# Relu tiles of their own for each score of the attention index, moved conv gates, and 68 instead of 60 early expert blocks

## The reference

```python
def conformer_conv(val, glu, conv_w, conv_vec):
    u = val * jax.nn.sigmoid(glu)
    ...
    return jax.nn.silu(layer_norm(y + conv_vec[0], conv_vec[1], conv_vec[2], LN_EPS))
    # its result is multiplied by silu of a third projection, the conv gate

def block(args):                       # dsa_attention, 128 queries
    idx_logits = jnp.einsum('bqhd,bsd->bqhs', qib, kf) * (IDX_HEAD_DIM ** -0.5)
    score = jnp.einsum('bqh,bqhs->bqs', wib * (IDX_HEADS ** -0.5), jax.nn.relu(idx_logits))
    adm = chunk_id[:, None, :] <= cqb[:, :, None]
    score = jnp.where(adm, score, -jnp.inf)
    top_val, top_idx = lax.top_k(score, k_sel)          # k_sel = 128
    ...                                # softmax attention of 16 heads over the chosen keys
```

## Time and profile before

| what | value |
|---|---|
| runs | 3465.48 us median of 3 (3461.9 to 3470.55) |
| profiled execution | 3471.03 us, its span 3468.7 us |
| busy share | PE 91%, DVE 64%, ACT 36%, POOL 25% |
| mean granted PE clock | 0.951 of full speed |

### The profile page before, as it was taken

The page is one execution under the profiler, slowest core; times in us unless marked ns, Lnnn a source line. Parts: engine busy times, 40 slices in busy tenths (PEclk is TensorE's granted clock), DMA queues, the critical chain, the costliest instruction groups (busy, mean ns, idle before and its releaser), DMA issues.

```text
span 3468.7 us, 39991 instructions
## 1 busy us (share of the span) xinstructions
PE 3142.5 (91%) x16218; PEld 2454.1 (71%) x16218; DVE 2206.1 (64%) x3495; ACT 1233.6 (36%) x1788; POOL 864.0 (25%) x540
## 2 busy tenths in 40 slices
PE   6799899997797799979899989979999999999996
PEld 4467677675585466757677778858888888888874
DVE  4689989753759766473679799746664444444445
ACT  3234344333322355323333356522222222222223
POOL 2344433320322211024335522222221111111100
PEclk9889999998898899989999999989999999999998
DMA  5211111325211111222223456665553333333330
GB/s 194 85 65 52 50 50 46 104 92 179 70 67 55 49 37 37 71 75 92 73 91 128 137 168 220 206 206 190 192 182 121 122 120 117 121 122 121 122 103 30
DMA packets 164950, 378.30 MB, mean 109 GB/s; under 512 B 10656, under 2 KB 77216, under 8 KB 164640
## 3 DMA queue, kind: packets, MB, share of 16 engines
q1 hardware_dynamic: 164768, 375.76, 32.2%
HBM read 318.04 MB, written 57.67 MB: 108 GB/s over the span
## 4 chain that ended last, share of the span: by engine, by line
PE 70%; DVE 22%; ACT 3%; DMA 2%; POOL 2%; issue 1%; SPq 0%; DVEq 0%; POOLq 0%; ACTq 0%
PE ps L651 20%; PE ps L653 19%; PE ps L652 19%; DVE rw L1648 5%; DVE oh L2197 2%; PE ps L1050 2%; PE ps L975 2%; PE ps L955 1%; DVE at L1936 1%; DVE ai L1934 1%; POOL wsp L2270 1%; PE ps L965 1%; POOL pk L2368 1%; PE ps L824 1%; DVE oh L2192 1%
## 5 line engine op out<-in xcount | busy, mean ns | idle before, releaser
L651 PE MATMUL ps<-hT,wsp 128*128 128x512 f32 x2120 | 878.5, 414 | 114.9 <-POOL wsp L2270 65.9
L653 PE MATMUL ps<-hT,wsp 128*128 128x512 f32 x2120 | 843.0, 398 | 0.0
L652 PE MATMUL ps<-hT,wsp 128*128 128x512 f32 x2120 | 842.6, 397 | 0.0
L2270 POOL TENSOR_TENSOR wsp<-ring,wsp 128x1024 fp32r<-128x1024 f32 x197 | 487.0, 2474 | 1142.9 <-ACT wsp L1109 1142.8
L651 PEld LDWEIGHTS ps<-hT,wsp 128*128 128x128 f32 x2120 | 408.9, 193 | 235.7 <-issue 79.8
L653 PEld LDWEIGHTS ps<-hT,wsp 128*128 128x128 f32 x2120 | 407.7, 192 | 90.2
L652 PEld LDWEIGHTS ps<-hT,wsp 128*128 128x128 f32 x2120 | 410.2, 193 | 80.4 <-issue 4.1
L2375 POOL TENSOR_TENSOR ex<-ex 128x512 fp32r<-128x512 f32 x128 | 175.4, 1385 | 894.5 <-ACT ex L1465 894.5
L2219 DVE TENSOR_TENSOR xT<-ps,xT 128x512 f32<-128x512 f32 x256 | 175.2, 688 | 285.2 <-PE ps L653 285.1
L1109 ACT ACTIVATE wsp<-ring 128x1024 fp32r<-128x1024 f32 x307 | 317.3, 1050 | 92.8 <-PE ps L653 68.3
L652 PE MATMUL ps<-ex 128*128 128x512 f32 x832 | 324.6, 390 | 0.0
(11 more groups left out here) (371 smaller groups left out, 4643.3 us busy)
## 6 DMA issues: line engine op xcount, KB each, us to landing
ring<-in_eu SPq DMA_DIRECT2D x128, 512.0 KB, 3.2
ring<-in_ev SPq DMA_DIRECT2D x128, 512.0 KB, 3.6
gd<-oh SPq DMA_DIRECT2D x8, 4096.0 KB, 14.4
ex<-gd SPq DMA_DIRECT2D x32, 1024.0 KB, 6.6
ring<-in_ein SPq DMA_DIRECT2D x57, 512.0 KB, 3.2
ring<-in_oin SPq DMA_DIRECT2D x40, 512.0 KB, 3.2
ring<-in_ada SPq DMA_DIRECT2D x37, 512.0 KB, 3.3
ex<-zd SPq DMA_DIRECT2D x15, 1024.0 KB, 9.0
```

The lines of the kernel that those rows point to most:

```text
L651: pe.matmul(out, W[0], R[0], start=first, stop=False)
L652: pe.matmul(out, W[0], R[1], start=False, stop=False)
L653: return pe.matmul(out, W[1], R[0], start=False, stop=last)
L2270: pool.tensor_tensor(s[:, 1, :], raw_of(i), s[:, 0, :].bitcast(F32), ALU.subtract).then_inc(pool_done, G.step("lo", i))
```

## The change

Seven edits. (1) The gates of conv planes 6 and 7 become pieces `late` behind the even output's fence, kept in `ag` and not sent through `yd`; `bgate` 7 is first in step 9. (2) `ybs` writes to tile `ya`, `yas` to tile `hT`, and `yas` k stands between the `lna` pieces; the tables' load is now `tab_in`. (3) Each of the 8 relu results of the index has its own tile; `selb` holds the mask (0 or a large negative number) from the `qi` pieces on and is the first summand, so `pick` has no mask operations. (4) `index` and `pick` of block 0 stand before `value`, those of block b + 1 before the next gate units; q runs one head further ahead. (5) 68 early blocks: three before `hot` 0 instead of one, 27 between `hot` 0 and `hot` 31 instead of 23, six instead of four from the stage's begin on. (6) `z` of units 0 to 3 stands before the last two of them, and each also splits and loads a unit of V. (7) The numbers of `PLACES` are others. The attention's output, the gate's transfers and all else stay.

```diff
--- before.py
+++ after.py
...
-NPRE = 15
+NPRE = 17
+LATE = 6
...
-    "first": (204, 310, 310, 310, 310, 311, 311, 311, 338, 338, 646, 683, 696, 704, 868, 868, 954),
...
+    "first": (135, 392, 392, 450, 593, 593, 679, 699, 699, 699, 879, 879, 927, 965, 976, 976, 976),
...
-        lane = [*(rkv(i) if i <= 7 else gates(range(3)) if i == 8 else gates(range(3, 8))),
+        lane = [*(rkv(i) if i <= 7 else gates(range(3)) if i == 8 else gates(range(3, LATE))),
                 *(x for g in mods.get(i, ()) for x in ada(1, g)),
-                *(dense("bgate", i - 2, 47 + i) if i >= 2 else []), *(conv_in(i + 1) if i <= 6 else [])]
+                *(dense("bgate", i - 2, 47 + i) if 2 <= i < 9 else []), *(conv_in(i + 1) if i <= 6 else [])]
+        if i == 9:
+            lane = [*dense("bgate", 7, 56), *lane]
...
+    order += [("late", m, unit("ein", 16 + m)) for m in range(LATE, 8)]
     order.append(("ybs",))
     order.append(("eb", 0, unit("eout", 1)))
     order.append(("lnm",))
@@ -242,7 +245,9 @@
         if m < 5:
             order.append(("eb", 3 + m, unit("eout", 2 * m + 7)))
         order.append(("lna", m))
-    order.append(("yas",))
+        if m >= 2:
+            order.append(("yas", m - 2))
+    order += [("yas", 6), ("yas", 7), ("tab_in",)]
...
     order.append(("ki", unit("oin", 22)))
+    order += [("qi", m, unit("oin", 18 + m)) for m in range(4)]
     order.append(("wi", unit("oin", 23)))
-    order += [("qi", m, unit("oin", 18 + m)) for m in range(4)]
     order.append(("key", unit("oin", 16)))
+    order.append(("index", 0))
+    order.append(("pick", 0))
     order.append(("value", unit("oin", 17)))
+    g = [0, 3, 7, 11, 16]
     for blk in range(4):
-        order.append(("index", blk))
-        if blk == 3:
-            order.append(("q", 0, unit("oin", 0)))
-        order.append(("pick", blk))
-        order += [("gate", m, unit("oin", 24 + m)) for m in range(4 * blk, 4 * blk + 4)]
+        order += [("gate", m, unit("oin", 24 + m)) for m in range(g[blk], g[blk + 1])]
+        if blk < 3:
+            order.append(("index", blk + 1))
+            if blk == 2:
+                order.append(("q", 0, unit("oin", 0)))
+            order.append(("pick", blk + 1))
+    order.append(("q", 1, unit("oin", 1)))
     for h in range(17):
         if h < 16:
             order.append(("logits", h))
         if h:
             order.append(("pt", h - 1))
-        if h < 15:
-            order.append(("q", h + 1, unit("oin", h + 1)))
+        if h < 14:
+            order.append(("q", h + 2, unit("oin", h + 2)))
...
+    for _ in range(3):
+        pre()
     for tb in range(S // TB):
-        if tb % 4 < 3:
+        if tb % 6 or tb == 30:
             pre()
         order.append(("hot", tb))
+
+    def zs(c):
+        return [("z", c, j, unit("eu", c * JC + j) if c >= NPRE else None) for j in range(JC)]
+
     order.append(("ex_begin",))
-    for _ in range(3):
-        pre()
+    pre()
+    pre()
     order.append(("gload", 0))
     pre()
     order.append(("gload", 1))
+    pre()
+    order.extend(zs(0))
+    pre()
+    pre()
     assert z[0] == NPRE * JC
     first = len(units)
-
-    def zs(c):
-        return [("z", c, j, unit("eu", c * JC + j) if c >= NPRE else None) for j in range(JC)]
-
-    order.extend(zs(0))
     for c in range(NC):
         if c + 1 < NC:
             order.extend(zs(c + 1))
...
+        relu = [*att[4:7], *att[10:14], small[:, :, :].rearrange("p a n -> p (a n)")]
...
+            def late(m, n):
+                w.wait_ge(tensor_done, T("use", n))
+                act.activation(ag[:, m, :], all_b.at[n], ACT.Silu).then_inc(scalar_done, A.step("ag", m))
...
-                    act.activation(hT[:, 0, k, :], yb[:, k, :], ACT.Copy).then_inc(scalar_done, A.step("yb", k))
+                    act.activation(ya[:, 0, k, :], yb[:, k, :], ACT.Copy).then_inc(scalar_done, A.step("yb", k))
...
-            def yas():
-                for k in range(8):
-                    w.wait_ge(pool_done, G("ya", k))
-                    act.activation(ya[:, 0, k, :], yc[:, k, :], ACT.Copy).then_inc(scalar_done, A.step("ya", k))
+            def yas(k):
+                w.wait_ge(tensor_done, T("free", "late"))
+                w.wait_ge(pool_done, G("ya", k))
+                act.activation(hT[:, 0, k, :], yc[:, k, :], ACT.Copy).then_inc(scalar_done, A.step("ya", k))
...
-                    w.wait_ge(vector_done, V.was("acc", (i - 3) // 8, (i - 3) % 8))
-                    act.activation(att[4 + i % 3], all_b.at["ix", blk, h], ACT.Relu, scale=0.125).then_inc(
+                    w.wait_ge(vector_done, V.was("acc", blk - 1, h))
+                    act.activation(relu[h], all_b.at["ix", blk, h], ACT.Relu, scale=0.125).then_inc(
...
+                if c == 0:
+                    hi_to(FIRST + j)
...
+                dve.tensor_scalar(selb[:, m, :], cidr, pcol[:, m:m + 1], NEG, ALU.is_gt, ALU.mult).then_inc(
+                    vector_done, V.step("late", m))
...
                 acc = att[7]
                 for h in range(8):
-                    x, wc = att[4 + (8 * blk + h) % 3], wi[:, blk * 8 + h:blk * 8 + h + 1]
                     w.wait_ge(scalar_done, A("relu", blk, h))
                     own()
-                    if h == 0:
-                        dve.tensor_scalar(acc, x, wc, None, ALU.mult).then_inc(vector_done, V.step("acc", blk, h))
-                    else:
-                        dve.scalar_tensor_tensor(out=acc, in0=x, scalar=wc, in1=acc, op0=ALU.mult,
-                                                 op1=ALU.add).then_inc(vector_done, V.step("acc", blk, h))
+                    dve.scalar_tensor_tensor(out=acc, in0=relu[h], scalar=wi[:, blk * 8 + h:blk * 8 + h + 1],
+                                             in1=acc if h else selb[:, blk, :], op0=ALU.mult, op1=ALU.add).then_inc(
+                        vector_done, V.step("acc", blk, h))
 
             def pick(blk):
-                acc, val, x = att[7], att[8], att[9]
-                dve.tensor_scalar(val, cidr, pcol[:, blk:blk + 1], None, ALU.is_le).then_inc(vector_done, V.step())
-                own()
-                dve.tensor_tensor(acc, acc, val, ALU.mult).then_inc(vector_done, V.step())
-                dve.tensor_scalar(x, val, -1.0, -NEG, ALU.add, ALU.mult).then_inc(vector_done, V.step())
-                own()
-                dve.tensor_tensor(acc, acc, x, ALU.add).then_inc(vector_done, V.step())
+
+                acc, x = att[7], att[9]
                 cur = acc
                 for _ in range(16):
                     own()
@@ -1936,12 +1954,10 @@
                     dve.match_replace(x, m8, cur, -3e38).then_inc(vector_done, V.step())
                     cur = x
                 own()
-                dve.tensor_tensor(x, x, acc, ALU.not_equal).then_inc(vector_done, V.step())
-                own()
-                dve.tensor_tensor(x, x, val, ALU.mult).then_inc(vector_done, V.step())
-                own()
-                dve.tensor_scalar(selb[:, blk, :], x, -1.0, -NEG, ALU.add, ALU.mult).then_inc(
-                    vector_done, V.step("sel", blk))
+                dve.tensor_tensor(x, x, acc, ALU.is_equal).then_inc(vector_done, V.step())
+                own()
+                dve.scalar_tensor_tensor(out=selb[:, blk, :], in0=x, scalar=NEG, in1=selb[:, blk, :], op0=ALU.mult,
+                                         op1=ALU.add).then_inc(vector_done, V.step("sel", blk))
...
+                if m < LATE:
+                    w.wait_ge(ag_in, 16)
+                else:
+                    w.wait_ge(scalar_done, A("ag", m))
...
-                for s in yt_out + ga_out:
+                for s in yt_out:
                     w.wait_ge(s, 64)
-                w.wait_ge(gs_out, 128)
+                for s in ga_out:
+                    w.wait_ge(s, 16 * LATE // 2)
                 for i in range(4):
+                    w.wait_ge(gs_out, 32 * (i + 1))
...
-                sp.dma_start(ag, t["yd"][16:24].rearrange("k p s -> p k s")).then_inc(ag_in, 16)
-
-            def yas():
+                sp.dma_start(ag[:, 0:LATE, :], t["yd"][16:16 + LATE].rearrange("k p s -> p k s")).then_inc(ag_in, 16)
...
+                elif c == 0:
+                    load_to(FIRST + j)
...
```

More of the change, by code:

```diff
@@ L592, in build @@
         one_unit = {"eb", "ea", "ki", "wi", "qi", "key", "value", "q", "gate", "oo", "pool_in", "bg", "cg", "vc", "wo", "wq",
-                    "pre", "ple"}
+                    "pre", "ple", "late"}
         def walk(pieces, split_to):
@@ L1088, in tensor_program @@
                   "norm2": lambda: T.here("free", "n2"), "ogs": lambda half: T.here("free", "ogs", half),
-                  "yas": lambda: T.here("free", "ya"), "ybs": lambda: T.here("free", "yb"),
+                  "late": late, "ybs": lambda: T.here("free", "late"),
                   "yms": lambda: T.here("free", "ym"),
@@ L2247, in vector_program @@
                   "p2": p2, "x1": x1, "st": st, "gnr": gnr, "gn4": gn4,
```

(2 more changed lines are left out.)

62 lines of the change are left out of this document (32 added, 30 removed).

## The result

The changed kernel takes 3389.43 us (median of 4, 3386.99 to 3394.37) against 3465.78 (median of 4) for the kernel before: a ratio of 0.9781, 95% interval 0.9764 to 0.9798, 76 us. Its profiled execution took 3389.65 us, 81.4 less than that of before. The forecast was 3380.

The account below looks back on a forecast made before the run. TensorE, busy 3142.5 of 3468.7 us, bounds the kernel; only its idle time and low clock can go. Terms -2 - 6 - 30 - 9.5 - 11.5 - 27 = -86 give 3385 for the execution, 3380 against the median; range 3348 to 3414.

Parts of the forecast that it names:

- A: Step 9 and even output: two conv gates moved behind the fence fill the 12.03 us gap; -2 us.
- B: Even output: yas between the lna pieces shortens the 7.78 us wait of ea 0; -6 us.
- C: Attention index: own relu tiles remove three TensorE gaps, VectorE's chain loses the mask operations; -30 us.
- E: Start of the expert stage: earlier gate-row load, six early blocks and splits within z remove idle and slow clock; -27 us.
- F: Steps 0 to 8: the new places move pieces by hundredths of a step; 0 us (-10 to +10).
- Nothing in the trace says which way that goes: Steps 0 to 8: the reason given for pricing the new places at 0 us.
- Rival 2: Steps: new places also remove half of each step's idle, 3 us in each of 7 steps; -107, 3358 us; chance 0.06.
- only a multiply, a copy and a subtraction stand behind the last lna: Even output: what remains before ea 0 after the change, about 2 us, from which the -6 us came.
- The sign given, L1942 with a mean under 1000 ns: Attention index: VectorE's multiply-adds would mean under 1000 ns if the index forecast held.
- the rival's -12: Attention index: POOL's splits hold VectorE up, so the index gives only 12 us; whole time 3409 us, chance 0.12.
- D: One-hot stage: more early blocks give -9.5 us before hot 0 and -11.5 us from hot 0 to hot 31.
- I leave 2.5 idle: Start of the expert stage: TensorE's idle time of 25.55 us would shrink to 2.5 us.

Follow-up runs that it names:

- e1: The kernel before with only the new numbers of PLACES; ratio 0.9958, 3450 us.
- e9: The kernel before with half of POOL's low part left out for the input projection's units from 30 on; ratio 0.9902, 3435 us.
- e4: The kernel before with only the even output's edits: late gates, bgate 7 first in step 9, ybs into ya, yas between lna pieces; ratio 1.0019, 3472 us.
- e10: The changed kernel with yas 3 to 7 behind lna 7 and the late gates undone, step 9's dense work ordered as before; ratio 0.9762.
- E6: The changed kernel with yas 3 to 7 behind lna 7 instead of between lna 5, 6 and 7; ratio 0.9795.

## Why the prediction came out as it did

The time, the direction and the range were right, and the closeness of the time is in part luck. A, B, C and E gave some 28 us less than forecast, and F gave 20 to 24 that no step of the prediction had. Two of the mechanisms (F, and that of B) were wrong; C and E were right in kind and wrong in size.

- **F, the new places: forecast 0, measured -22.5 by e1's trace and about -20 over all traces.** The step that failed is "Nothing in the trace says which way that goes". The trace did show what there was to gain: VectorE was busy 423.97 of 473.9 us, its L1648 means 996 ns over the page where L1630, of the same form, takes 744, and L1690, 128 x 3, took 2.2 us right before the 2.29 of rows 8. What it could not show is which wait the new places would remove: the taps' mean stayed (997 over the page of the change), and L1690's went. I held the idle time of TensorE against the places and did not ask what VectorE's busy time held. Rival 2 had the size (3 us a step; the trace has 2.7) with a chance of 0.06, and e9 and the rows of steps 3 to 6 show what is behind some 11 us of it, a wait of VectorE inside POOL's splits; another 5 are clock in step 1.
- **A and B: forecast -8, measured +2.5 (e4 alone +5.3).** A's steps were right (step 9 at 47.3, a gap of 5.5 before late 7, 3.6 before eb 0), its gain of 2 was not there: eb 0 begins 72.4 us behind step 8 for 71.6, and e10 has 0.7 for the gates. In B "only a multiply, a copy and a subtraction stand behind the last lna" failed. Behind lna 5, 6 and 7 each plane goes through DVE, ACT, POOL, ACT and DVE in turn, and the normalisation of a plane stands in VectorE's queue behind the subtraction of an earlier one, which waits for ACT: a plane takes 3.34 us. E6 gives 3.9 of the 8 back; what is left of B's 6 and A's 2 was not looked into.
- **C: forecast -30, measured -20.8, alone -21.7.** The mechanism was right, three sizes were off. Counted from the stage's begin, the first sum comes 6.5 sooner, not 11. The sums take 36.9 us for 26.7, 10.2 more and not 8.6: half of the splits met a sum, as said, but a meeting costs 1.8 us and not 1.2. And the queries' begin and end cost 8.5, not 7 (a gap of 2.44 behind logits 1 and gaps of 3.38 and 3.23 at the end, where before had one of 3.37). The sign given, L1942 with a mean under 1000 ns, did not come: it is 1210. The truth lies between the term and the rival's -12.
- **D: forecast -21, measured -22.2.** Right by its steps: 2.02 before hot 0, and 246.5 from the end of hot 0 to hot 31, where 248 was said against 237.5 (the table's 250.6 and 241.9 have hot 0 in them). PE is busy 0.975 of it (over 0.98 was said).
- **E: forecast -27, measured -18.6.** The load goes at +17.5 (2228.73 less 2211.2), where 16 to 17 was said. The first product is ready 14.3 us behind that load and not 12.7, but still 2 us before the early blocks end, so v 0 starts at once, at +34. What failed is the term "I leave 2.5 idle" with full clock: v 0 takes 32.07 us for 21.9, 6.25 idle and the rest slow clock, since its later units wait for splits that stand between the multiplies, with their weights landing only just in time.

The range was summed up from half widths that come to 24 us, which is 3356 to 3404 and not the 3354 to 3408 that stands there; the final range is wider, and nothing hangs on it.

## What to carry to other kernels

When an engine that sets the pace shows operations of one kind at two lengths, count the longer ones against the other engine's long operations before pricing a reordering at nothing: here shifts of a few hundredths of a step were worth some 20 us, half of it through one small operation in four steps, and the moved gates and copies together cost 2.5. When work is interleaved between two in-order engines, write down the round that each item makes; several items back to back cost one pass, alternating ones a round each. And after an early transfer, price the whole row of work behind its landing, not the first product, and the landings of the other inputs of that work beside it.
